# Gated networks of a two-block transformer kernel: a second chunk through seven block products for eight, weight sums made in DRAM, one stream of weight blocks

## The chip, the cores and the metric

One NeuronCore of a Trainium2 chip runs the whole program. The metric is device time in microseconds from start to end of one execution, taken as the median over runs. Engines are PE (TensorE), DVE (VectorE), ACT (ScalarE), POOL (GpSimd) and SP (SyncE, which only issues DMAs here).

## The reference, cut to what matters

Two transformer blocks are applied to 512 tokens of width 1024. The first has a mixer, a cross-attention and a two-matrix network (D_FF 4096). The second has a gated network, a token mixer with two kinds of attention, and a second gated network. The change touches the gated networks:

```python
def swiglu(h, w1, w3, w2):                     # w1, w3: 1024 x 2816, w2: 2816 x 1024
    return (jax.nn.silu(h @ w1) * (h @ w3)) @ w2

h = rmsnorm(x, ffn1_norm[l])
x = x + 0.5 * swiglu(h, ffn1_w1[l], ffn1_w3[l], ffn1_w2[l])
...
h = rmsnorm(x, ffn2_norm[l])
x = x + 0.5 * swiglu(h, ffn2_w1[l], ffn2_w3[l], ffn2_w2[l])
return rmsnorm(x, final_norm[l])
```

All is float32. The kernel makes each product of three reduced-precision products: an operand is split in a high part (rounded to fp32r) and a low part (the rest), and high*high, high*low and low*high are added in PSUM.

## The kernel before, in words

**Layout.** Activations lie with features on the partitions: 8 tiles (KT) of 128 features by 512 tokens (T). `h` is the running sum; `xh`/`xl` and `ah`/`al` are two pairs of high and low parts, one for a layer's input and one for its hidden values. A **panel** is 1024 rows by 256 columns (PC) of a weight matrix, 1 MB. SP loads it into one of two halves of `raw`, ACT rounds it into `wh` (`conv`, or `hi` by halves), and DVE subtracts to get `wl` (`conv`, `lo`); panel p uses half p % 2 of all three. PE then runs 2 output tiles x 8 k tiles x 3 matmuls of 512 columns (`panel_t`). SP issues a load when the panel two before has been converted (`conv_done`), ACT converts when PE has finished the panel two before (`lin_done`). Every engine works through its own list in program order and waits on counting semaphores.

**Order of panels.** `P0` numbers the panels: fqk, fv, gqk, gv, gr (mixer of block one, woven with attention), xk and xv (keys and values of the memory, 256 tokens wide, so that PE needs half the columns for them), wout, xq, xo, mlp, ffn1, then `SEQ` (block two's mixer, q0 ... v3, nq0 ... ga3, woven with attention), mnsa, wout2, ffn2. Between the fourth and fifth load of xv and wout, SP also issues the two reloads of `h` (L608, L610), 1 MB each, on the same queue.

**A gated network.** The 2816 hidden columns are cut in a tail of 768 and two chunks of 1024. The tail is done by plain panels: 6 of w1 and w3, then 4 panels of w2 with 6 k tiles. Each chunk r = 1, 2 is a **phase**: four groups, then four plain panels of w2 (three of them counted here for the last one in ffn2; the fourth is woven into the end of the kernel).

**A group** does 256 columns of w1 and of w3 together as a 2 x 2 block product in seven products for eight. A block is 512 rows by 256 columns of weights (4 k tiles) against 256 tokens. A product is 2 output tiles x 4 k tiles x 3 = 24 matmuls of 256 columns.

```python
B11, B21, B22, T1, T2, T3, T4 = range(7)
A11, A12, A22, S3, S1, S2, S4 = range(7)
PRODUCTS = [(A11, B11, 0), (A12, B21, 2), (S2, T2, 0), (S3, T3, 1), (S1, T1, 0), (A22, T4, 1), (S4, B22, 0)]
```

The third number says which of the group's three PSUM banks takes the product; two groups alternate between the banks `ps0, ps1, pt1` (shown by the profile as score, score, turned) and `po0, po1, pt0` (mix, mix, turned). T1 to T4 are sums of token quarters, made once for a network (`token_parts`, kept in `XS_h`, `XS_l`). S1 to S4 are sums of weight quarters, made for each group by DVE in the raw buffers (`sum_1` to `sum_4`, `add_up`, L3022), between the conversions of the blocks (`block_high` on ACT, `block_low` on DVE). SP loads four quarters of 512 KB for each group (L630), into `raw` or into the spare room of `xl_f` or `al_f`. ACT copies partial results out (`kept`), DVE adds them (`made_11`, `made_22`, `made_21`), ACT applies Silu, DVE multiplies (`gate`), and both write the high and low parts of the hidden values. In `in_turn`, product 6 of a group comes after product 0 of the next.

GpSimd has no work in this kernel, and no DMA comes from its queue.

Of the kernel before, what the change touches and what calls it, by code (L numbers as in the profile page):

```python
# [11 lines left out]
PART = 128  # L12
# [26 lines left out]
for name_, count_ in (("small", 1), ("fqk", 4), ("fv", 2), ("gqk", 2), ("gv", 2), ("gr", 2), ("xk", 4), ("xv", 4),  # L39
                      ("wout", 4), ("xq", 4), ("xo", 4), ("mlp", 20), ("ffn1", 18),  # L40
                      ("mix2", 32), ("mnsa", 8), ("wout2", 4), ("ffn2", 18)):
    P0[name_] = at
    at += count_
# [59 lines left out]
MLP0 = {"mlp": 2, "ffn1": 2 + 8 + 24, "ffn2": 2 + 8 + 24 + 22}  # L103
ML_S0 = MLP0["ffn1"]
# [7 lines left out]
for name_, chunks_, groups_ in (("mlp", 3, 2), ("ffn1", 2, 4), ("ffn2", 2, 4)):  # L112
    for r_ in range(1, chunks_ + 1):
        PHASES[name_, r_] = (at, groups_, P0[name_] + (8 if name_ == "mlp" else 10) + 4 * (r_ - 1))
        at += groups_
# [160 lines left out]
def build(nc, d, out):  # L276
    ctx = ExitStack()
    with ctx:
# [3399 lines left out]
```

## Time and profile before

| what | us |
|---|---|
| median of 3 runs | 2136.93 (2136.85 to 2138.73) |
| the profiled execution | 2138.95 |
| its span, first to last instruction | 2137.2 |
| PE busy | 2118.8 (99%) |
| DVE busy | 1372.5 (64%) |
| ACT busy | 1032.6 (48%) |

The span is what the rows below lie in. The profiled execution took 1.75 us more than its span and lies 2.0 us above the median. Busy PE means that a matmul is in flight: matmuls overlap, so a matmul of 256 columns is shown at 281 ns though the next one starts some 118 ns later. How long a stretch takes is read from its ends, not from these durations.

### The profile page before, as it was taken

To read this page: it belongs to the slowest core of one execution; us is meant where nothing else is said; L and a number is where in the kernel's file an instruction comes from. 1 tells how busy PE (TensorE), PEld (TensorE's weight loads), DVE (VectorE), ACT (ScalarE), POOL (GpSimd) and SP (SyncE) were. 2 spreads that over 40 slices of the span, in tenths; PEclk is the share of its full clock that TensorE was granted. 3 is DMA by queue.
4 is the path that set the end of the run, shared out by engine and by line. 5 is a ranking of instruction groups with operands and counts; after the bars stand their busy time and mean duration, and the time that the engine had idled before them with its cause. 6 is when DMAs were issued, how large, how long until landed. Compare 5 with 4: busy or idle time off the path is not lost.

```text
span 2137.2 us, 32530 instructions
## 1 busy us (share of the span) xinstructions
PE 2118.8 (99%) x13100; PEld 1819.8 (85%) x13100; DVE 1372.5 (64%) x2281; ACT 1032.6 (48%) x1738; POOL 0.2 (0%) x4
## 2 busy tenths in 40 slices
PE   9999999999999999999999999999999999999999
PEld 7888988888998988898988888887777888899997
DVE  4664663467664767775856777647776356686674
ACT  6654545543533543453543565546666234354344
POOL 0000000000000000000000000000000000000000
PEclk9999999999999999999999999999999999999999
DMA  5121522133233132424323622321111233242421
GB/s 189 60 80 60 180 97 80 40 99 118 80 119 118 61 98 84 138 75 138 100 80 98 181 83 82 98 84 50 40 37 40 79 99 99 87 139 72 138 68 71
DMA packets 190920, 199.74 MB, mean 93 GB/s; under 512 B 8481, under 2 KB 185778, under 8 KB 190258
## 3 DMA queue, kind: packets, MB, share of 16 engines
q1 hardware_dynamic: 190770, 197.66, 29.2%
q8 instruction: 104, 1.70, 0.3%
q14 instruction: 46, 0.38, 0.1%
HBM read 188.73 MB, written 2.10 MB: 89 GB/s over the span
## 4 chain that ended last, share of the span: by engine, by line
PE 93%; DVE 3%; ACT 2%; issue 1%; DMA 1%; SPq 0%; DVEq 0%; ACTq 0%
PE lin L733 20%; PE lin L735 19%; PE lin L734 19%; PE mix L1279 3%; PE mix L1280 3%; PE mix L1281 3%; PE score L1279 3%; PE score L1280 3%; PE score L1281 3%; PE turned L834 3%; PE score L929 3%; PE mix L943 2%; PE turned L1279 1%; PE turned L1280 1%; PE turned L1281 1%
## 5 line engine op out<-in xcount | busy, mean ns | idle before, releaser
L733 PE MATMUL lin<-xh,wh 128*128 128x512 f32 (+1 forms) x1032 | 407.5, 395 | 1.7 <-DVE wl L2494 1.2
L735 PE MATMUL lin<-xh,wl 128*128 128x512 f32 (+1 forms) x1032 | 394.8, 383 | 0.0
L734 PE MATMUL lin<-xl,wh 128*128 128x512 f32 (+1 forms) x1032 | 393.7, 382 | 0.0
L733 PE MATMUL lin<-ah,wh 128*128 128x512 f32 (+1 forms) x788 | 308.5, 392 | 1.4 <-DVE al L2499 0.6
L735 PE MATMUL lin<-ah,wl 128*128 128x512 f32 (+1 forms) x788 | 306.0, 388 | 0.0
L734 PE MATMUL lin<-al,wh 128*128 128x512 f32 (+1 forms) x788 | 305.9, 388 | 0.0
L2488 DVE TENSOR_TENSOR wl<-raw,wh 128x2048 fp32r<-128x2048 f32 x85 | 194.8, 2292 | 123.7 <-ACT wh L1595 123.7
L733 PEld LDWEIGHTS lin<-xh,wh 128*128 128x128 f32 x1032 | 194.2, 188 | 45.4 <-issue 9.6
L735 PEld LDWEIGHTS lin<-xh,wl 128*128 128x128 f32 x1032 | 194.0, 188 | 39.0
L734 PEld LDWEIGHTS lin<-xl,wh 128*128 128x128 f32 x1032 | 194.5, 188 | 34.8 <-issue 1.0
L1595 ACT ACTIVATE wh<-raw 128x2048 fp32r<-128x2048 f32 x85 | 162.0, 1906 | 113.4 <-PE lin L735 106.4
L733 PEld LDWEIGHTS lin<-ah,wh 128*128 128x128 f32 x788 | 148.0, 188 | 33.2 <-issue 1.6
L735 PEld LDWEIGHTS lin<-ah,wl 128*128 128x128 f32 x788 | 147.9, 188 | 30.7
L734 PEld LDWEIGHTS lin<-al,wh 128*128 128x128 f32 x788 | 148.0, 188 | 30.1 <-issue 0.2
L2494 DVE TENSOR_TENSOR wl<-raw,wh 128x1024 fp32r<-128x1024 f32 x90 | 109.5, 1220 | 40.4 <-ACT wh L1602 39.9
L2602 DVE CUSTOM_DVE_ANT_0 arena<-score,cst 128x128 f32<-128x128 f32 (+2 forms) x224 | 97.6, 486 | 58.0 <-PE score L929 46.6
L1692 ACT ACTIVATE arena<-arena,negm 128x128 f32<-128x128 f32 (+2 forms) x224 | 122.8, 555 | 3.1 <-DVE negm L2602 3.0
L1680 ACT ACTIVATE arena<-turned 128x512 f32<-128x512 f32 (+1 forms) x128 | 68.8, 582 | 112.5 <-PE turned L834 112.2
L1602 ACT ACTIVATE wh<-raw 128x1024 fp32r<-128x1024 f32 x90 | 94.1, 1052 | 36.1 <-PE lin L735 23.8
L1280 PE MATMUL mix<-arena_r,wh 128*128 128x256 f32 x352 | 98.9, 281 | 0.0
L1281 PE MATMUL mix<-arena_r,wl 128*128 128x256 f32 x352 | 98.9, 281 | 0.0
L1279 PE MATMUL mix<-arena_r,wh 128*128 128x256 f32 x352 | 98.9, 281 | 0.0
(434 smaller groups left out, 4301.1 us busy)
## 6 DMA issues: line engine op xcount, KB each, us to landing
raw<-in_w_in_dram SPq DMA_DIRECT2D x38, 1024.0 KB, 5.3
raw<-in_ffn_w_dram SPq DMA_DIRECT2D x28, 1024.0 KB, 5.2
raw<-in_mlp_w_dram SPq DMA_DIRECT2D x20, 1024.0 KB, 5.2
raw<-in_ffn_w_dram SPq DMA_DIRECT2D x32, 512.0 KB, 4.8
raw<-in_xattn_wkv_dram SPq DMA_DIRECT2D x8, 1024.0 KB, 5.3
raw<-in_w_out_dram SPq DMA_DIRECT2D x8, 1024.0 KB, 5.3
xl_f<-in_ffn_w_dram SPq DMA_DIRECT2D x16, 512.0 KB, 6.0
al_f<-in_ffn_w_dram SPq DMA_DIRECT2D x16, 512.0 KB, 5.5
```

The lines of the kernel that those rows point to most:

```text
L733: nc.tensor.matmul(o, w[0], x[0], start=first, stop=False)
L734: nc.tensor.matmul(o, w[0], x[1], start=False, stop=False)
L735: return nc.tensor.matmul(o, w[1], x[0], start=False, stop=last)
L1279: nc.tensor.matmul(o[:, c, :], left_h[:, k, cols], XS_h[:, b, k, :], start=begins, stop=False, skip_group_check=True)
L1280: nc.tensor.matmul(o[:, c, :], left_h[:, k, cols], XS_l[:, b, k, :], start=False, stop=False, skip_group_check=True)
L1281: mm = nc.tensor.matmul(o[:, c, :], left_l[:, k, cols], XS_h[:, b, k, :], start=False, stop=k == HT - 1, skip_group_check=True)
L1595: nc.scalar.activation(wh[:, p % 2], raw[:, p % 2], ACT.Copy).then_inc(hi_done, 1)
L1602: nc.scalar.activation(wh[:, p % 2, :, cols], raw[:, p % 2, :, cols], ACT.Copy).then_inc(hi_half[c], 1)
L1692: op = nc.scalar.activation(PB[:, s % 2, a, col:col + nk], SM[:, a, col:col + nk], ACT.Exp, bias=negm[:, at:at + 1], scale=-1.0, accum_out ...
L2488: nc.vector.tensor_tensor(wl[:, p % 2], raw[:, p % 2], wh[:, p % 2].bitcast(F32), ALU.subtract).then_inc(conv_done, 1)
L2494: nc.vector.tensor_tensor(wl[:, p % 2, :, cols], raw[:, p % 2, :, cols], wh[:, p % 2, :, cols].bitcast(F32), ALU.subtract).then_inc(conv_d ...
L2602: op = nc.vector.tensor_tensor_reduce(out=SM[:, a, col:col + nk], in0=ps[a][:, col:col + nk], in1=mask, scale=scale, scalar=BIG, op0=ALU.a ...
```

## The change

1. **The down product of the first chunk** (w2 rows of chunk 1, all 1024 output columns) is no longer four plain panels but two sets of seven block products: quarters of w2 are 4 k tiles by 512 columns. Its right-hand blocks are the hidden values, in quarters B11, B21, B22 (`hidden_at`) and sums T1 to T4, which DVE makes as the values come (`turned`) and ACT and DVE split (`U_T`, `turned_low`). Each product's PSUM is added to `h` straight away by DVE (`added`), with scale 0.5 or -0.5.
2. **Weight sums** S1 to S4 are no longer made by DVE. A new program on GpSimd makes them in DRAM, for all 1024 (or 512) columns of a chunk at once: a copy, then DMAs that add to what lies there (`accum_op`). Eight steps for each of UP, DOWN and LAST, 24 for each network, each waiting for the one before (`su`). A step moves 2 MB (UP, LAST) or 1 MB (DOWN). Those of ffn1 begin when PE has finished all panels before fv, those of ffn2 when it has finished all before nq0.
3. **One stream.** The ten sets (4 UP, 2 DOWN, 4 LAST) are one list of 70 blocks. Every block, sums too, is loaded by SP (512 KB), into six raw buffers in turn, and split into a ring of five (`ring_at`; one of the five is a new place in the arena). Then come the four (or three) plain panels of the second chunk.
4. Panels fall from 18 to 14 for each gated network, and several counts are renumbered.

```diff
+UP, DOWN, LAST = range(3)
+SETS = [(UP, i_) for i_ in range(4)] + [(DOWN, i_) for i_ in range(2)] + [(LAST, i_) for i_ in range(4)]
+STREAM = in_turn(4) + [(4, n_) for n_ in (0, 3, 1, 2, 4, 5)] + [(5, 0), (4, 6)] + [(5, n_) for n_ in (3, 2, 1, 4, 5)]
+STREAM += [(6, 0), (5, 6)] + [(i_ + 6, n_) for i_, n_ in in_turn(4)[1:]]
+BLOCKS, RINGS, RAWS = len(STREAM), 5, 6
+SUM_STEPS = 24
+SUMS_FROM = {"ffn1": P0["fv"], "ffn2": P["nq0"]}
...
         @block.sync
...
-                for r in range(1, 3):
-                    phase(name, r, p0 + 6, w2[:, (r - 1) * KT:r * KT])
+                p = p0 + 10
+                for b in range(BLOCKS):
+                    if b >= RAWS:
+                        sp.wait_ge(st_l, block_count(name, b - RAWS))
+                    elif b < 2:
+                        sp.wait_ge(lin_done, 2 * (p0 + 6))
+                    else:
+                        sp.wait_ge(conv_done, p if b < 4 else p - 1)
...
+                    if sums_ready(name, b):
+                        sp.wait_ge(su, sums_ready(name, b))
+                    sp.dma_start(raw_at(name, b), block_source(name, b)).then_inc(landed_b, 16)
...
+        @block.gpsimd
+        def _(pool):
+
+            def step(n, dst, src, **kw):
+                if n:
+                    pool.wait_ge(su, 16 * n)
+                pool.dma_start(dst, src, **kw).then_inc(su, 16)
+
+            for name in GATED:
+                pool.wait_ge(lin_done, 2 * SUMS_FROM[name])
+                for what in (UP, DOWN, LAST):
+                    n = SUM_STEPS * GATED.index(name) + 8 * what
+                    a11, a12, a21, a22 = quarters(name, what)
+                    s3, s1, s2, s4 = sums_of(name, what)
+                    step(n, s3, a11)
+                    step(n + 1, s3, a21, accum_op=ALU.add)
+                    step(n + 2, s1, a21)
+                    step(n + 3, s1, a22, accum_op=ALU.add)
+                    step(n + 4, s2, s3)
+                    step(n + 5, s2, a22, accum_op=ALU.add)
+                    step(n + 6, s4, s2)
+                    step(n + 7, s4, a12, accum_op=ALU.add)
...
         @block.tensor
...
+            def stream(name):
...
+                for b, (s, n) in enumerate(STREAM):
+                    what = SETS[s][0]
+                    if s == 4 and n in (3, 1):
+                        continue
+                    if s == 4 and n == 0:
+                        pe.wait_ge(ml_lo, hidden_count(name, 2, 3))
+                        for n_ in (0, 3, 1):
+                            pe.wait_ge(st_l, block_count(name, AT[s, n_]))
+                            bank_free(s, n_)
+                            part(s, n_, range(HT - 1))
+                        pe.wait_ge(ml_lo, hidden_count(name, 3, 3))
+                        for n_ in (0, 3, 1):
+                            part(s, n_, [HT - 1]).then_inc(st_q, 1)
+                        continue
+                    pe.wait_ge(st_l, block_count(name, b))
+                    if n in (0, 1, 3):
+                        bank_free(s, n)
+                    elif what == DOWN:
+                        pe.wait_ge(st_c, event_count(name, s, {2: 0, 4: 2, 5: 3, 6: 4}[n]))
...
+                    part(s, n, range(HT)).then_inc(st_q, 1)
...
-                phase(name, 1, Y)
-                phase(name, 2, Y, 3 if name == "ffn2" else 4)
+                stream(name)
+                outputs(p0 + 10, Y, lambda k: pe.wait_ge(ml_lo, hidden_count(name, 6 + k // 2, 2)), 3 if name == "ffn2" else 4)
...
         @block.scalar
...
+                for b, (s, n) in enumerate(STREAM):
...
+                    elif what == UP and n == 6:
+                        high(hidden_at(name, 0, B22)[:, i, :], E_ur[:, 1, :], s, 2)
+                        act.wait_ge(st_a, turned_count(name, i, 4))
+                        nc.scalar.activation(US[name][0][1][:, 0:4, i, :], U_T, ACT.Copy).then_inc(ml_hi, 1)
...
+                def turned(i):
+                    dve.wait_ge(ml_e, 2 * MLP_G + gate_count(name, i, 2))
...
+                    nc.vector.tensor_tensor(U_T[:, T3 - T1, :], b12, b22, ALU.subtract).then_inc(st_a, 1)
...
+                    nc.vector.tensor_tensor(U_T[:, T2 - T1, :], U_T[:, T3 - T1, :], b11, ALU.subtract).then_inc(st_a, 1)
...
+                    nc.vector.tensor_tensor(U_T[:, T4 - T1, :], b21, U_T[:, T2 - T1, :], ALU.add).then_inc(st_a, 1)
+                    nc.vector.tensor_tensor(U_T[:, 0, :], b11, b12, ALU.subtract).then_inc(st_a, 1)
...
+                def added(s, n, i):
...
+                    dve.wait_ge(st_q, product_count(name, s, n))
...
+                    nc.vector.scalar_tensor_tensor(hk, half_bank(s, at), scale, hk, ALU.mult, ALU.add).then_inc(st_c, 1)
...
+                for b, (s, n) in enumerate(STREAM):
+                    what, i = SETS[s]
+                    up = what != DOWN
+                    if not up:
+                        added(s, n, i)
...
+                    if b + RINGS < BLOCKS:
+                        stream_low(name, b + RINGS)
```

**DVE, from the fourth UP set to the first DOWN set.** Before, at the end of the first phase (L3136 is a gate, L3067 a `made`, L2499 a low part, L2488 a panel's low part, L2551 the add into `h` from a plain panel):

```order
L3067 TENSOR_TENSOR arena<-mix,arena 128x512 [waits st_e,st_q]
L3136 TENSOR_TENSOR arena<-arena 128x512 [waits ml_s,st_c]
L2499 TENSOR_TENSOR al<-arena,ah 128x2x256 [waits ml_hi]
L3136 TENSOR_TENSOR arena<-arena 128x512 [waits ml_s,st_c]
L2499 TENSOR_TENSOR al<-arena,ah 128x2x256 [waits ml_hi]
L2488 TENSOR_TENSOR wl<-raw,wh 128x2048 [waits hi_done]
L2551 SCALAR_TENSOR_TENSOR h<-lin,h 128x512 [waits lin_done] x2
```

Now, at the same place (L3365 is the gate, L3376 to L3381 are `turned`, L2722 a low part, L3399 is `added`):

```order
L3365 TENSOR_TENSOR arena<-arena 128x512 [waits ml_s,st_c]
L3376 TENSOR_TENSOR arena<-arena 128x256 [waits ml_lo,ml_e]
L3378 TENSOR_TENSOR arena<-arena 128x256 [waits st_a]
L3380 TENSOR_TENSOR arena<-arena 128x256 [waits st_a]
L3381 TENSOR_TENSOR arena<-arena 128x256
L2722 TENSOR_TENSOR xl<-arena,xh 128x256 [waits ml_hi]
L2722 TENSOR_TENSOR al<-arena,ah 128x4x256 [waits ml_hi]
L2722 TENSOR_TENSOR wl<-raw,wh 128x1024 [waits st_h]
L3399 SCALAR_TENSOR_TENSOR h<-score,h 128x2x256 [waits st_q]
L2722 TENSOR_TENSOR wl<-raw,wh 128x1024 [waits st_h]
L3399 SCALAR_TENSOR_TENSOR h<-score,h 128x2x256 [waits st_q]
L2722 TENSOR_TENSOR wl<-raw,wh 128x1024 [waits st_h]
```

Four small sums and a wide low part stand behind the last gate, and in the DOWN sets each product's add into `h` is followed by the low part of a block that is used five products later.

**POOL, its whole list before:**

```order
L3667 ISA
L3667 MEMSET const-float32-0.0 128x1
L3667 MEMSET const-float32-1.0 128x1
L3667 MEMSET const-bfloat16-1.0 128x1
L3667 MEMSET const-uint8-127 128x1
```

Now, behind the same five, the steps of ffn1 up to the first of LAST (`up_sums_ffn_0` are the sums of the first chunk, `down_sums_ffn` those of w2):

```order
L876 DMA up_sums_ffn_0<-in_ffn_w_2_dram 128x4x1024 [waits lin_done]
L876 DMA up_sums_ffn_0<-in_ffn_w_2_dram 128x4x1024 [waits su] x3
L876 DMA up_sums_ffn_0<-up_sums_ffn_0 128x4x1024 [waits su]
L876 DMA up_sums_ffn_0<-in_ffn_w_2_dram 128x4x1024 [waits su]
L876 DMA up_sums_ffn_0<-up_sums_ffn_0 128x4x1024 [waits su]
L876 DMA up_sums_ffn_0<-in_ffn_w_2_dram 128x4x1024 [waits su]
L876 DMA down_sums_ffn<-in_ffn_w_2_dram 128x4x512 [waits su] x4
L876 DMA down_sums_ffn<-down_sums_ffn 128x4x512 [waits su]
```

Each step is one DMA from DRAM to DRAM and waits for all of the one before. None of them waits for, or holds up, a compute engine directly; they share the DMA engines with SP's loads.

## Rows read from the trace of the kernel before

**Rows 1.** The page: busy engines, and the queue of SP's loads.

```profile
PE 2118.8 (99%) x13100; PEld 1819.8 (85%) x13100; DVE 1372.5 (64%) x2281; ACT 1032.6 (48%) x1738; POOL 0.2 (0%) x4
...
q1 hardware_dynamic: 190770, 197.66, 29.2%
```

**Rows 2.** Waits of PE: line, whom it waited for, us, times, longest.

```profile
PE score L1279 <- DVE wl L2499: 1.2, 2, 0.8
```

**Rows 3.** Windows: us, PE, PEld, DVE, ACT, POOL busy, clock, DMA share, GB/s.

```profile
884.00:964.00 80.00, 79.19 (x673) 78.98 (x672) 65.44 (x68) 41.24 (x51) 0.00 (x0) 1.00 0.27 85
1007.60:1087.30 79.70, 79.70 (x673) 79.70 (x672) 62.97 (x66) 40.32 (x50) 0.00 (x0) 1.00 0.27 85
1879.00:1960.30 81.30, 80.87 (x674) 80.65 (x673) 65.18 (x67) 41.19 (x51) 0.00 (x0) 1.00 0.27 84
2003.90:2083.60 79.70, 79.70 (x674) 79.70 (x673) 62.95 (x66) 40.41 (x50) 0.00 (x0) 1.00 0.27 85
964.00:1007.60 43.60, 43.60 (x195) 36.08 (x194) 20.51 (x19) 11.52 (x10) 0.00 (x0) 1.00 0.42 136
```

**Rows 4.** Groups of instructions between 1007.6 and 1087.3 us (the second phase).

```profile
L2499 DVE TENSOR_TENSOR wl<-xl_f,wh 128x1024 fp32r<-128x1024 f32 x10 | 12.2, 1220 | 3.6 <-ACT wh L2055 3.6
L2055 ACT ACTIVATE wh<-xl_f 128x1024 fp32r<-128x1024 f32 x10 | 10.5, 1054 | 9.1 <-DVE xl_f L3022 4.9 <-PE mix L1281 3.6 <-PE score L1281 0.7
L3022 DVE TENSOR_TENSOR xl_f<-xl_f 128x1024 f32<-128x1024 f32 x8 | 9.8, 1220 | 0.1
```

**Rows 5.** The line of one token sum: durations in ns.

```profile
L3001 DVE TENSOR_TENSOR arena<-arena x12: 425/425/426, 476.3 to 1846.4; 128x256 f32<-128x256 f32 x12
```

**Rows 6.** Timeline where the second phase's last product ends: start us, us, engine.

```profile
1087.32 0.39 PE L733 MATMUL lin<-ah,wh 128*128 128x512 f32 x1
...
1087.52 0.60 ACT L2133 ACTIVATE arena<-mix 128x512 f32<-128x512 f32 x1 [6.15 <-PE mix L1281]
...
1089.27 0.68 DVE L3136 TENSOR_TENSOR arena<-arena 128x512 f32<-128x512 f32 x1
```

**Rows 7.** Windows in the memory's values and the output projection.

```profile
222.00:272.00 50.00, 50.00 (x399) 49.07 (x398) 29.83 (x32) 24.73 (x36) 0.00 (x0) 1.00 0.63 211
246.60:258.10 11.50, 11.50 (x98) 11.50 (x97) 2.85 (x2) 5.50 (x6) 0.00 (x0) 1.00 0.96 345
```

**Rows 8.** Timeline of SP, ACT and DVE there.

```profile
246.13 0.37 SPq L577 DMA_DIRECT2D raw<-in_xattn_wkv_dram  x1
246.54 0.58 SPq L608 DMA_DIRECT2D h<-in_x_t_dram  x1
247.16 0.43 SPq L610 DMA_DIRECT2D h<-in_x_t_dram  x1
254.10 0.38 SPq L577 DMA_DIRECT2D raw<-in_w_out_dram  x1
...
261.37 1.90 ACT L1595 ACTIVATE wh<-raw 128x2048 fp32r<-128x2048 f32 x1
267.13 1.91 ACT L1595 ACTIVATE wh<-raw 128x2048 fp32r<-128x2048 f32 x1
...
263.30 2.29 DVE L2488 TENSOR_TENSOR wl<-raw,wh 128x2048 fp32r<-128x2048 f32 x1 [3.47 <-ACT wh L1595]
```

**Rows 9.** DMA between 1719 and 1726 us: queues, and the issue with its us to landing.

```profile
q8 instruction: 1, 0.02, 1.7%
...
raw<-in_w_out_dram SPq DMA_DIRECT2D x1, 1024.0 KB, 6.7
```

**Rows 10.** The page: DMA issues, KB each, median us to landing.

```profile
raw<-in_w_out_dram SPq DMA_DIRECT2D x8, 1024.0 KB, 5.3
...
arena<-arena SPq DMA_DIRECT2D x104, 64.0 KB, 2.0
```

**Rows 11.** Timeline of ACT where the new steps' start conditions are met.

```profile
70.64 1.91 ACT L1595 ACTIVATE wh<-raw 128x2048 fp32r<-128x2048 f32 x1
...
1362.57 1.05 ACT L1602 ACTIVATE wh<-raw 128x1024 fp32r<-128x1024 f32 x1
```

More of the change, by code:

```diff
@@ L101 @@
 HEAD_TILES = [0, 4, 1, 5, 2, 6, 3, 7]
[L103 to L104 removed]
+MLP0 = {"mlp": 2, "ffn1": 2 + 8 + 24, "ffn2": 2 + 8 + 24 + 26}
+GATE0 = {"ffn1": 0, "ffn2": 22}
 TAIL = 3
@@ L111 @@
 PHASES, at = {}, 0
[L112 to L115, printed above, removed]
+for r_ in range(1, 4):
+    PHASES["mlp", r_] = (at, 2, P0["mlp"] + 8 + 4 * (r_ - 1))
+    at += 2
 GROUPS = at
@@ new lines, in build, with quarters, sums_of @@
+        down_sums = {name: nc.dram_tensor(f"down_sums_{name}", (4, HT * PART, 2 * PC), F32, kind="Internal").ap() for name in GATED}
+        def quarters(name, what):
+            w1, w3, w2 = ffw[name]
+            if what == DOWN:
+                return [w2[:, e:KT:2, c * 2 * PC:(c + 1) * 2 * PC] for c in range(2) for e in range(2)]
+            r = what // LAST
+            return [w[:, e * HT:(e + 1) * HT, r * D:(r + 1) * D] for w in (w1, w3) for e in range(2)]
+        def sums_of(name, what):
+            store = down_sums[name] if what == DOWN else up_sums[name, what // LAST]
+            return [tiles(store[k]) for k in range(4)]
@@ new lines, in own, with raw_at, ring_at @@
+        def own(name):
+            return (P0[name] + 10) % 2
+        def raw_at(name, b):
+            at = b % RAWS
+            if at < 2:
+                return ((ah_f, al_f) if name == "ffn2" else (xh_f, xl_f))[at][:, 3]
+            side = own(name) if at >= 4 else 1 - own(name)
+            return raw[:, side, at % 2 * HT:(at % 2 + 1) * HT, :]
+        def ring_at(name, b):
+            at = b % RINGS
+            if at == 0:
+                return RING_h, RING_l
+            side = own(name) if at < 3 else 1 - own(name)
+            at = (at - 1) % 2
+            return tuple(x[:, side, at * HT:(at + 1) * HT, :] for x in (wh, wl))
@@ L549, in build, with hidden_at, set_banks, half_bank @@
+        def hidden_at(name, side, b):
+            left, turned = US[name][side]
+            return left[:, b] if b < T1 else turned[:, b - T1]
+        def set_banks(s):
+            return ((ps[0], ps[1], pt[1]), (po[0], po[1], pt[0]))[s % 2]
+        def half_bank(s, at):
+            return set_banks(s)[at].rearrange("p (a n) -> p a n", a=2)
         block = ctx.enter_context(nc.Block())
@@ L1296, in phase, with outputs @@
+            def outputs(p, Y, made, panels=4):
                 s = p % 2
@@ L3210, in rest @@
                 last()
-            chunk("mlp", p + 4, 1.0, {0: third, 1: fourth, 2: fifth})
+            early, later, last = first_blocks(PHASES["mlp", 1][0])
+            residual(p + 4, None, None, 1.0, 2, {0: third, 1: fourth, 2: fifth, 5: early, 6: later})
+            last()
             for r in range(1, D_FF // D):
```

339 lines of the change are left out of this document (213 added, 126 removed).

## The prediction

> **What bounds the kernel now.** I read the page first: PE is busy 99% of the span, DVE 64%, ACT 48%, and SP's queue uses 29.2% of the DMA engines [rows 1]. So the time is PE's list of matmuls plus the gaps in it, and anything else counts only where it makes PE wait. Next the waits of PE: inside the gated networks there are just two, together 1.2 us, both for the low part of a block at the start of a first phase [rows 2]. Then the windows by stage: a phase of 28 products (672 matmuls of 256 columns) takes 80.0, 79.7, 81.3 and 79.7 us, and the four plain panels between two phases (192 matmuls of 512 columns) take 43.6 us [rows 3]. That is 79.7 / 672 = 0.1186 us and 43.6 / 192 = 0.2271 us for a matmul. DVE is busy 63 to 65 us in 80, so it is the engine nearest to PE there. The DMA engines are busy 27% in a phase.
>
> **The sum for PE's list.** Removed for each network: 192 matmuls of 512 columns. Added: 14 products x 24 = 336 matmuls of 256 columns, 336 x 0.1186 = 39.85 us. The stream has 70 x 24 = 1680 matmuls, 199.25 us at that pace. Before, the same work took 80.0 + 43.6 + 79.7 = 203.3 us in ffn1 and 81.3 + 43.6 + 79.7 = 204.6 us in ffn2. So -4.05 and -5.35, together **-9.4 us**. This takes with it the two waits of [rows 2], which I expect to go: block 0 no longer waits for the last tail panel's buffer and there are no sums to make between the first blocks. About 1 us of it is that ffn2's first phase ran slower than the others; I don't know why, and count on the usual pace.
>
> **DVE's list.** A sum of a block costs 1.22 us; there were 4 for each group, 16 in a phase, so 32 x 1.22 = 39 us of DVE goes for each network [rows 4]. Added are 4 UP sets x 4 small sums x 0.425 us [rows 5] and the wide low part, 1.22 us. DVE gets lighter, but that was hidden under PE and gives nothing.
>
> **The turn from UP to DOWN.** Where the fourth UP set ends, the hidden values' sums are late next. Before, after a last product ACT starts Silu 0.20 us after PE went on, takes 0.60, and a gate takes 0.68 [rows 6]. The chain now: 0.2 + 0.6 + 0.7 + 4 x 0.43 for `turned` + 1.05 for ACT's copy of `U_T` + 1.22 for DVE's low part [rows 4 to 6] + some 0.2 for hand-overs = 5.7 us. PE meanwhile does 3 products without their last k tile, 54 x 0.1186 = 6.4 us. So no wait, with 0.7 us to spare; if the cover were gone it would cost up to 1 us a network.
>
> **Behind the turn there is one.** In the first DOWN set product 4 uses the PSUM bank of product 2 and follows it directly (0, 3, 1, 2, 4, 5), so PE must wait for `added` of product 2. DVE is behind then. I count from the end of the last UP product: `turned_low` ends at 5.6, the next block's low part at 6.75. Products 0, 3, 1 end at 7.1, 7.8, 8.55, nearly at once. DVE then does three times `added` (0.65, as the 512-element gate of [rows 6]) and a block's low part (1.15 back to back), whose high part ACT can only start when the product has freed the ring: 7.3 to 9.6, to 11.35, to 13.1. `Added` of product 2 ends at 13.8, but PE ended that product at 8.55 + 2.85 = 11.4. Wait: 2.4 us, twice, **+4.8 us**. Bounds: 1.0 us each if DVE is free at once (hand-over and 0.7), 3.5 each if every block adds another 0.3. In the other DOWN set a product of another set lies between the two. From there to the plain panels, `conv(p)` waits for product 67 of 70, 5.7 us before the end, and needs 1.9 + 2.3 us [rows 8]: hidden.
>
> Both together: -9.4 + 4.8 = **-4.6 us**, if the DMAs cost nothing.
>
> **The steps on GpSimd.** They are off every engine, so their price is only what they take from SP's loads. The trace has no DRAM-to-DRAM DMA and none that adds. The nearest row for data is 345 GB/s in a stretch where the engines are 96% busy [rows 7], for the fixed part 2.0 us of a 64 KB DMA [rows 10]. A copied step of 2.1 MB: 6.1 + 2.0 = 8.1 us. For an adding step the lower bound is the same (8.1), the upper three passes (read what is there, read what is added, write): 20.3. I take two passes, 14.2. With halves for DOWN: UP 4 x 22.3 = 89, DOWN 4 x 13.1 = 52, LAST 89, in all 230 us. The steps of ffn1 begin at 70.6, when PE has finished the panels ahead of fv [rows 11]: LAST would run from 212 to 301 us. At the lower bound all 24 take 170 us and end at 240, a bit later because the loads share.
>
> The Trainium skill (Collectives: The Full Stack, "The bandwidth ceiling") says that a reducing DMA needs two source reads and so runs at half a copy's rate; that is what I took, and no row here shows it. Its page DMA: Bandwidth & Descriptors ("Anatomy of one DMA") gives 2.0 us + bytes / 436 GB/s for a GpSimd DMA; with that and the halved rate LAST would run from 189 to 263 us, and the sum below would end 2.6 us lower.
>
> **Who is hurt.** A load hardly matters where its data lie ready long before conversion. The one stretch where they don't is xk, xv and wout: the panels of the memory need half the columns, and the DMA engines are busy 63% over 50 us and 96% from 246.6 to 258.1 [rows 7]. SP issues at 246.13, 246.54, 247.16 and 254.10 four MB in a row [rows 8]; 4.2 MB at 345 GB/s and 2.0 us fixed end at 260.3. The last of them is wout's first panel: ACT converts it at 261.37, DVE ends at 265.6, PE starts it when it has finished the one before, 267.13, where ACT starts the next conversion [rows 8]. So slack is 1.1 + 1.5 = 2.6 us. As the DMA engines have no free time there, what the steps move is added one for one. I take one adding step, 12.2 us of data: 12.2 - 2.6 = 9.6, and with what the xv panels before it lose **+10.5 us**. Bounds: nothing (steps over, or the arbiter favours SP), and two adding steps of three passes with the copy between, 2 x 18.3 + 6.1 = 42.7, less the 18.5 us that the engines are idle in those 50: 24.
>
> That a load suffers from another queue is in the trace: one packet of the instruction queue, 1.7% of 16 engines x 7 us = 1.9 us on one engine, made a load land after 6.7 us where the median is 5.3 [rows 9, 10]. The skill's DMA page ("Queues, rings and completion order") says that each engine takes turns between queues by packets. With SP's 1 KB against 4 KB rows of the sums, SP would get a small share while a step runs, which leans to the upper half of my bounds.
>
> ffn2's steps begin at 1362.57 [rows 11] and would end near 1593, with loads that wait for conversion anyway, long before 1879 [rows 3]. I count 0 for them, up to 10 us if a load queued ahead of the small rotations' DMAs is late.
>
> **Sum:** -9.4 + 4.8 + 10.5 = +5.9 us. Against the profiled execution's 2138.95 this is 2144.8; that execution lies 2.0 above the median of the runs shown, so I forecast 2142.8.
>
> **Rivals.** About 0.2% (4.3 us) is what a measurement of this kernel can tell from no change.
> - *A, forecast: the steps of LAST collide with the loads of xv and wout, for more than 8.9 us.* For it: 63% and 96% DMA share. Time 2141.2 to 2157, likeliest 2142.8. Chance 0.43.
> - *B: they collide, but cost only 3 to 8.9 us,* because adding steps have long idle parts in which SP catches up. 2135.3 to 2141.2, say 2138. Chance 0.19.
> - *C, the other side: no collision that counts.* It decides itself at 246.13: 24 steps in 175 us, 7.3 us each, while my lower bound is 170 us. Or SP's small packets pass ahead. Then -4.6 us: 2132.3; with a DOWN wait of 1.0 us each 2129.5. Chance 0.32, of which 0.22 below 2132.7 and 0.10 just within 0.2%.
> - *D: adding is far slower.* LAST's first sum of ffn2 is loaded about 33 products into the stream, 1879 + 94 = 1973. From 1362.57 that is 25 us for each step, 2.6 times what I took (230 / 24 = 9.6). Beyond that PE waits for sums, and the steps lie over all loads of both halves: +25 us and more, 2162 and up. Chance 0.06.
>
> **Chances.** Slower: A 0.43 + D 0.06 = 0.49. Faster: 0.22 of C, and 0.04 of B where the DOWN wait is smaller too: 0.26. Same: 0.25. Range: below 2129 lie some 0.07 (C with a faster pace of matmuls), above 2160 D and the end of A, 0.10. So 2129 to 2160. The forecast case alone is 2141 to 2157.
>
> **What would show it.** In the trace of the changed kernel: the stream at 199 us plus one gap of about 2.4 us before the fifth product of the first DOWN set, ended by DVE's `added`; no gap at its start; none at the turn. GpSimd's DMAs from 70 to about 300 us and from 1363 to 1600. Loads of xv and wout that land after 8 to 17 us instead of 5.3, and PE idle between 235 and 285 us by about 10 us. I am wrong if PE is not idle there, if the steps end before 246, or if the gaps in the stream sum to another size.

## The result, and the profile after

The changed kernel takes **2161.98 us** (median of 4 runs, 2160.51 to 2163.58) against 2136.90 (4 runs, 2136.85 to 2138.73): ratio 1.0115, 95% interval 1.0098 to 1.0133. It is 25 us slower, where I had forecast 5.9 and a range up to 2160. The profiled execution took 2162.04 with a span of 2159.5, 22.3 more than the span of before.

The page of the changed kernel: busy engines, queues (packets, MB, share of 16 engines), DMA issues (KB each, median us to landing; the 24 are 8 copies and 16 additions).

```profile
PE 2119.8 (98%) x13388; PEld 1833.4 (85%) x13388; DVE 1348.2 (62%) x2289; ACT 1053.8 (49%) x1766; POOL 49.0 (2%) x52
...
q1 hardware_dynamic: 222578, 229.12, 33.6%
q0 software_dynamic: 23296, 83.89, 15.9%
...
up_sums_ffn<-in_ffn_w_dram POOLq DMA_DIRECT2D x24, 2048.0 KB, 14.1
...
up_sums_ffn<-up_sums_ffn POOLq DMA_DIRECT2D x8, 2048.0 KB, 9.4
```

PE has 288 matmuls more than in [rows 1], short ones for long ones, and is busy 1.0 us longer. The span grew by 22.3, so the loss is idle time, and what the idle time does to PE's busy time. Its waits in the changed kernel: line, whom it waited for, us, times, longest.

```profile
PE lin L900 <- DVE wl L2711: 9.2, 2, 5.5
PE score L1460 <- DVE h L3399: 4.7, 2, 2.3
PE turned L1001 <- DVE arena L3643: 4.1, 1, 4.1
PE lin L900 <- DVE arena L2753: 2.9, 1, 2.9
```

The pair of waits in [rows 2] is gone. In its place stand four kinds. The waits behind L2711 and L2753 end at 244.01, 269.54 and 282.51 us: VectorE is named, but it had waited, through ScalarE, for a load. L3399 is `added` in the first DOWN set of each network. L3643 lies at 1403, which nothing in my sum had. The windows show what the page can't (us, PE, PEld, DVE, ACT, POOL busy, clock, DMA share, GB/s):

```profile
235.00:300.00 65.00, 52.90 (x334) 49.05 (x333) 22.20 (x23) 20.82 (x27) 4.76 (x5) 0.89 1.02 319
...
244.00:247.00 3.00, 2.99 (x14) 3.00 (x15) 3.00 (x5) 0.00 (x0) 0.00 (x0) 0.50 0.49 199
250.00:253.00 3.00, 3.00 (x27) 3.00 (x26) 0.93 (x1) 0.47 (x1) 0.00 (x0) 1.00 1.12 252
993.40:995.70 2.30, 0.04 (x1) 0.00 (x0) 2.30 (x4) 1.06 (x1) 0.00 (x0) 1.00 0.74 241
996.00:999.00 3.00, 3.00 (x27) 3.00 (x27) 0.84 (x2) 0.03 (x1) 0.00 (x0) 1.00 0.86 279
1998.30:2001.30 3.00, 3.00 (x16) 3.00 (x16) 0.06 (x1) 0.00 (x1) 0.00 (x0) 0.50 1.01 311
```

In 235 to 300 us the DMA engines have no free time (1.02; 0.63 and 0.96 in [rows 7]), and PE is idle for 12.1 us of 65. Right behind the first wait the granted clock is 0.50, the lower of the two levels (1.2 GHz): 14 matmuls in 3 us instead of 27. PE counts as fully busy there. So a wait costs more than its length: three waits of 12.1 us in all cost 18.4. The same at 1998, behind a wait of 2.3 us; behind the like wait at 995.7 the clock stayed at 1.00.

Where the time went I read from the moments at which PE ends the same panel in two traces. Each column is the difference to the kernel before, in us; the last line is the difference of the spans. What a column shows in its first line stands there from the first panel on, so it is an offset of the start. The execution that all columns are taken from lies 2.0 us above the median of its kernel, so the last line flatters every variant by up to that much: e9 is 10.0 lower there and 7.9 in the medians.

| end of | before, at | changed | e8 | e1 | e3 | e7 | e9 |
|---|---|---|---|---|---|---|---|
| xk's third panel | 238 | +0.3 | -0.2 | -0.3 | -0.6 | -0.4 | -0.4 |
| xk's last panel | 244 | +4.8 | +4.7 | -0.3 | +3.9 | +5.1 | -0.4 |
| xv's last panel | 267 | +10.3 | +11.1 | -0.3 | +10.9 | +5.1 | -0.4 |
| wout's second panel | 290 | +18.7 | +19.3 | -0.3 | +18.9 | +5.1 | -0.4 |
| ffn1's tail (the stream starts) | 884 | +18.6 | +19.2 | +4.2 | +18.7 | +5.0 | -0.5 |
| ffn1 and the next panels | 1137 | +16.4 | +19.0 | +2.1 | +14.0 | +0.3 | -5.2 |
| SEQ up to nq0 | 1375 | +17.9 | +18.8 | +3.7 | +15.3 | +0.8 | -3.8 |
| the first delta attention panel | 1415 | +23.8 | +19.8 | +10.6 | +16.9 | +0.8 | -3.8 |
| ffn2's tail (the stream starts) | 1879 | +24.6 | +21.1 | +10.6 | +16.9 | +1.0 | -3.6 |
| the span | 2137.2 | +22.3 | +19.6 | +8.2 | +10.4 | -5.4 | -10.0 |

The changed kernel: 18.4 lost beside xv and wout (4.5 by the end of xk, 5.5 in xv, 8.4 in wout's first panel), 2.3 gained by ffn1, 1.5 lost at about 1200, 5.9 at 1400, 0.8 at about 1570, 2.3 gained by ffn2.

**The first place.** GpSimd's issues, then ACT and SP, in the changed kernel (start us, us):

```profile
226.49 1.26 POOL L876 DMA_DIRECT2D down_sums_ffn<-in_ffn_w_dram  x1 [5.42 <-DMA down_sums_ffn<-down_sums_ffn]
236.49 0.76 POOL L876 DMA_DIRECT2D up_sums_ffn<-in_ffn_w_dram  x1 [8.74 <-DMA down_sums_ffn<-in_ffn_w_dram]
247.44 1.25 POOL L876 DMA_DIRECT2D up_sums_ffn<-in_ffn_w_dram  x1 [10.19 <-DMA up_sums_ffn<-in_ffn_w_dram]
263.69 0.76 POOL L876 DMA_DIRECT2D up_sums_ffn<-in_ffn_w_dram  x1 [15.00 <-DMA up_sums_ffn<-in_ffn_w_dram]
276.48 1.24 POOL L876 DMA_DIRECT2D up_sums_ffn<-in_ffn_w_dram  x1 [12.03 <-DMA up_sums_ffn<-in_ffn_w_dram]
...
258.94 26.67 SPq L704 DMA_DIRECT2D raw<-in_w_out_dram  x4
...
265.25 1.91 ACT L1800 ACTIVATE wh<-raw 128x2048 fp32r<-128x2048 f32 x1 [4.71 <-DMA raw<-in_xattn_wkv_dram]
278.18 1.91 ACT L1800 ACTIVATE wh<-raw 128x2048 fp32r<-128x2048 f32 x1 [10.29 <-DMA raw<-in_w_out_dram]
```

LAST begins at 236.5, not at 212, and its fourth step is issued at 276.5. Wout's first panel, issued at 258.94, lands at 278.2. The DMA view of this load, in the kernel before (issued at 254.10) and in the changed one (KB, us to landing):

```profile
raw<-in_w_out_dram SPq DMA_DIRECT2D x1, 1024.0 KB, 6.5
raw<-in_w_out_dram SPq DMA_DIRECT2D x1, 1024.0 KB, 19.2
```

ACT had waited 10.3 us for it. Three steps lie over this one load, one of them issued ahead of it and two while it runs; I had counted one. Xv's last load takes 14.3 us where it took 5.6, and ACT waits 4.7 us for it.

How hard a step crowds SP's loads differed with its kind. Queues in the changed kernel (packets, MB, share of 16 engines), first from 252 to 258.9 us, inside an adding step, then from 263.7 to 276.5, a copied one. SP has three loads outstanding in the first stretch and two or more in the second:

```profile
q0 software_dynamic: 316, 1.29, 95.1%
q1 hardware_dynamic: 184, 0.19, 10.0%
...
q1 hardware_dynamic: 1406, 3.17, 63.0%
q0 software_dynamic: 528, 2.10, 39.8%
```

Beside the adding step SP's queue (q1) moves 0.19 MB in 6.9 us, beside the copy 3.17 MB in 12.8. That stretch is the worst of the adding step; over all of it, 247.4 to 263.7 us, SP's queue has 38.8%.

**The second place,** at 1399 us: SP's swap of the first sparse query tile's halves (64 KB DMAs), VectorE behind it, PE behind that.

```profile
1393.66 2.41 SPq L825 DMA_DIRECT2D arena<-arena  x4
...
1398.21 0.69 DVE L3524 TENSOR_TENSOR arena<-arena,cst 128x512 f32<-128x512 f32 x1 [5.36 <-DMA arena<-arena]
...
1403.32 0.66 PE L1001 MATMUL turned<-cst,arena 128*128 128x128 f32 x4 [4.10 <-DVE arena L3643]
```

And from the DMA view of that moment (KB each, us to landing):

```profile
arena<-arena SPq DMA_DIRECT2D x1, 64.0 KB, 5.8
```

A 64 KB DMA takes 5.8 us beside an adding step, 2.0 in [rows 10]. VectorE's instruction that needs it stands ahead of the one that PE needs, and PE waits 4.1 us for a value that has nothing to do with the swap.

### The profile page after: what moved, and what is told of

It reads as the page before. It is cut to its first block, busy times and chain, and to the rows that moved or that the text cites. A ratio compares the mean times of both kernels' runs of the same rounds, so it can differ in the third digit from the quotient of the medians.

```text
span 2159.5 us, 33285 instructions
## 1 busy us (share of the span) xinstructions
PE 2119.8 (98%) x13388; PEld 1833.4 (85%) x13388; DVE 1348.2 (62%) x2289; ACT 1053.8 (49%) x1766; POOL 49.0 (2%) x52
## 4 chain that ended last, share of the span: by engine, by line
PE 89%; DVE 4%; DMA 3%; ACT 2%; issue 1%; SPq 0%; DVEq 0%; ACTq 0%
PE lin L900 18%; PE lin L902 17%; PE lin L901 17%; PE mix L1461 3%; PE mix L1462 3%; PE mix L1460 3%; PE score L1460 3%; PE score L1461 3%; PE score L1462 3%; PE turned L1001 3%; PE score L1096 2%; PE mix L1110 2%; DMA raw<-in_w_out_dram 1%; PE turned L1461 1%; PE turned L1462 1%
## 5 line engine op out<-in xcount | busy, mean ns | idle before, releaser
L900 PE MATMUL lin<-xh,wh 128*128 128x512 f32 (+1 forms) x968 | 384.1, 397 | 5.8 <-DVE arena L2753 2.9
L902 PE MATMUL lin<-xh,wl 128*128 128x512 f32 (+1 forms) x968 | 371.2, 383 | 0.0
L901 PE MATMUL lin<-xl,wh 128*128 128x512 f32 (+1 forms) x968 | 370.0, 382 | 0.0
L900 PE MATMUL lin<-ah,wh 128*128 128x512 f32 x724 | 284.9, 393 | 6.9 <-DVE wl L2711 5.5
L902 PE MATMUL lin<-ah,wl 128*128 128x512 f32 x724 | 282.0, 390 | 0.0
L901 PE MATMUL lin<-al,wh 128*128 128x512 f32 x724 | 281.9, 389 | 0.0
L2711 DVE TENSOR_TENSOR wl<-raw,wh 128x2048 fp32r<-128x2048 f32 x77 | 176.5, 2292 | 127.8 <-ACT wh L1800 127.8
L2722 DVE TENSOR_TENSOR wl<-raw,wh 128x1024 fp32r<-128x1024 f32 x88 | 107.0, 1222 | 47.5 <-ACT wh L2340 46.3
L2717 DVE TENSOR_TENSOR wl<-raw,wh 128x1024 fp32r<-128x1024 f32 x90 | 109.5, 1221 | 42.2 <-ACT wh L1807 41.7
L1807 ACT ACTIVATE wh<-raw 128x1024 fp32r<-128x1024 f32 x90 | 94.1, 1052 | 46.4 <-PE lin L902 26.0
L2340 ACT ACTIVATE wh<-raw 128x1024 fp32r<-128x1024 f32 x74 | 77.7, 1055 | 61.1 <-PE score L1462 19.5
L900 PE MATMUL lin<-wh,xh 128*128 128x256 f32 x320 | 93.3, 292 | 3.8 <-DVE wl L2711 3.8
```

What stands on the lines that cost most here:

```text
L900: nc.tensor.matmul(o, w[0], x[0], start=first, stop=False)
L901: nc.tensor.matmul(o, w[0], x[1], start=False, stop=False)
L902: return nc.tensor.matmul(o, w[1], x[0], start=False, stop=last)
L2711: nc.vector.tensor_tensor(wl[:, p % 2], raw[:, p % 2], wh[:, p % 2].bitcast(F32), ALU.subtract).then_inc(conv_done, 1)
L2717: nc.vector.tensor_tensor(wl[:, p % 2, :, cols], raw[:, p % 2, :, cols], wh[:, p % 2, :, cols].bitcast(F32), ALU.subtract).then_inc(conv_d ...
L2722: nc.vector.tensor_tensor(dst, full, hi.bitcast(F32), ALU.subtract).then_inc(done, 1)
```

## The experiments

Theory 1: the loss is that of place, sums beside loads that have no slack. Theory 2: the sums cost as much wherever they lie. Theory 3: the new stream of products costs it. Theories 1 and 2 are told apart by moving sums, 3 by leaving them out. The differences by place that I name are those of the table or read in the same way.

### e1: ffn1's sums later

```diff
-SUMS_FROM = {"ffn1": P0["fv"], "ffn2": P["nq0"]}
+SUMS_FROM = {"ffn1": P0["xq"], "ffn2": P["nq0"]}
```

> Only the start of ffn1's 24 sums moves, from the second panel of FoX's v projection (70 us) to the xattn query projection (about 340 us), behind the stage in which PE waited. Theory 1 (place): the 18.4 us that the changed kernel falls behind between 235 and 300 us come from the loads of xv, wout and xq standing in line with the sums, so they go and nothing takes their place, because the loads of xo and of the mlp's panels have more slack: 2143.5, 2140 to 2146. Theory 2 (the sums cost wherever they lie): the same number of bytes meets other loads; the loss moves to 400 to 600 us and the time stays at 2158 to 2163. Theory 3 (the new stream of products is what costs, the waits at 240 to 280 being its effect by some other way): no change, 2162.

2148.37 (2147.12 to 2150.71), before 2138.18 (19 runs), ratio 1.0050 (1.0033 to 1.0067): above the 2140 to 2146 that I expected. The 18.4 us are gone to the last tenth (-0.3 at 290 us). But 4.7 came back at 540 us, so theory 1 holds with a part of theory 2 in it: the sums met the mlp's first group loads, which have no slack either. The loss at 1400 was 6.9 this time.

### e2: no sums

```diff
-        @block.gpsimd
-        def _(pool):
...
-                    if sums_ready(name, b):
-                        sp.wait_ge(su, sums_ready(name, b))
-                src = sums_of(name, what)[SUM[a] - 1]
+                src = quarters(name, what)[SUM[a] - 1]
```

> The 48 sum steps and the waits for them are left out; the blocks that were sums are read straight from a quarter of the weight instead, so the output is not the reference's, but PE, VectorE, ScalarE and SP's own loads do all the work of the changed kernel. Theory 1: all of the loss is DMA traffic, what is left is the shorter list of products (-9.4) and the two 2.3 us waits in the first set of the down product with up to 1.7 us of half clock behind the second: 2132 to 2135, 2 to 5 us below the kernel before. Theory 3 (the new stream costs more than its matmuls): above 2140. If the waits for the sums themselves (blocks late for the stream) cost anything it shows as a difference between this run and the one with both sets of sums moved.

2135.44 (10 runs), before 2138.18, ratio 0.9988 (0.9979 to 0.9997): 0.4 above the 2132 to 2135 that I expected, 2.7 below the kernel before. The span is 2132.4, 4.8 below before, where my sum without the DMAs had -4.6; 1.4 of the 4.8 is a slow phase in the trace of before (see e8). Theory 3 falls.

### e3: the order of the first DOWN set

```diff
-[(4, n_) for n_ in (0, 3, 1, 2, 4, 5)]
+[(4, n_) for n_ in (0, 3, 1, 2, 5, 4)]
```

> In the first set of the down product, products 4 and 5 change places, so that the one that adds to the bank of product 2 no longer follows it at once. Everything else is the changed kernel. Theory 1 (my step on VectorE's wait): both waits of 2.3 us on h go, and so does the 3.4 us stretch of half clock at 1998 us: 4.6 to 6.5 us less than the changed kernel, 2155.5 to 2157.5. Rival: the VectorE chain of sixteen instructions behind the end of the up product is what is late, and the wait only moves to product 5 or to the next set: within 1 us of the changed kernel, 2161 to 2162.5.

2153.66 (2150.21 to 2155.86), ratio 1.0071 (1.0056 to 1.0086). Both waits are gone, and nothing stands in their place. Ffn1 gives 4.7 (18.7 to 14.0) instead of 2.3. The median is 8.3 below the changed kernel, 1.8 more than I expected at most. The profiled execution is the fastest of the four (2150.21), and it lost 1.6 at 1399 us instead of 5.9; what the other three lost there, no trace shows. E11 prices the order without this. The DVE rows of the changed kernel show the wait:

```profile
992.07 1.22 DVE L2722 TENSOR_TENSOR wl<-raw,wh 128x1024 fp32r<-128x1024 f32 x1
993.20 0.68 DVE L3399 SCALAR_TENSOR_TENSOR h<-turned,h 128x512 f32<-128x512 f32 x1
993.80 1.22 DVE L2722 TENSOR_TENSOR arena_r<-raw,arena_r 128x1024 fp32r<-128x1024 f32 x1
994.93 0.68 DVE L3399 SCALAR_TENSOR_TENSOR h<-score,h 128x512 f32<-128x512 f32 x1
...
995.76 0.36 PE L1460 MATMUL score<-ah,wh 128*128 128x256 f32 x1 [2.33 <-DVE h L3399]
```

VectorE works without a gap, an addition and a low part in turn, and PE gets its bank back when the fourth addition ends.

### e4: both sums later, and the new order

```diff
+SUMS_FROM = {"ffn1": P0["xq"], "ffn2": P["wda0"]}
+[(4, n_) for n_ in (0, 3, 1, 2, 5, 4)]
```

> Three edits in one: ffn1's sums from the xattn query projection, ffn2's sums two panels later (from the first output panel of the delta attention instead of the first query panel of the sparse attention, so that the swap of the first query tile is ahead of them), and the order of the down product as in the run before. Theory 1: 18.4 + about 6 + 4.6 to 6.5 us less than the changed kernel: 2131 to 2133.5, 4 to 6 us below the kernel before. Theory 2 (sums cost wherever they lie): 2150 or more. If ffn2's sums meet the later swaps in the same way, the second part stays and it is 2137 to 2139.

2134.11 (10 runs), ratio 0.9981 (0.9972 to 0.9990): 4.1 below the kernel before, where I expected 4 to 6, and 0.6 above the expected 2131 to 2133.5. PE's longest wait:

```profile
PE score L1440 <- DVE wl L2722: 3.6, 1, 3.6
```

This is the mlp's first group, at 540 to 544 us: 5.0 with the half clock behind it, 4.7 in e1. The wait at 1399 is gone (+0.0 there).

### e7: only ffn1's LAST steps later

The rest as in e4, but ffn1's sums begin at `P0["fv"]` as in the change.

```diff
+                    if name == "ffn1" and what == LAST:
+                        pool.wait_ge(lin_done, 2 * P0["xq"])
```

> The order of the down product of e3 and ffn2's start of e4, but ffn1's sums start where the change put them (70 us); only the eight steps of its LAST set are held back to the xattn query projection (about 335 us). The eight UP and eight DOWN steps lie between 70 and 235 us, where the changed kernel lost 0.3 us; the LAST steps lie between 335 and about 425, ahead of the mlp's first group loads at 510 to 518, which cost e4 its one stall (3.9 us and a 3.4 us stretch of half clock, 4.8 in the milestones). Theory 1 (place: it is a question of which loads the sums lie beside): e4 less 4.8, so 2129.3, 2128 to 2131. Theory 2 (a sum costs the same anywhere): 2134, and a stall in the xattn stage between 335 and 425.

2134.70 (11 runs), ratio 0.9984 (0.9976 to 0.9993). My expectation of 2129.3 was a miss: the mlp's wait went, but a wait at 240 stayed, which with the half clock behind it cost 5.5 us (-0.4 to +5.1):

```profile
PE lin L902 <- DVE arena L2755: 3.8, 1, 3.8
```

I had read "0.3 lost until 235" as no harm, but the harm of the last DOWN step shows only behind 235. (The 0.3 is no loss at all, but the offset of the start.) Rows of e7's timeline, and its DMA view for that load (KB, us to landing):

```profile
227.13 1.26 POOL L876 DMA_DIRECT2D down_sums_ffn<-in_ffn_w_dram  x1 [5.72 <-DMA down_sums_ffn<-down_sums_ffn]
...
229.13 22.50 SPq L704 DMA_DIRECT2D raw<-in_xattn_wkv_dram  x4
...
239.05 1.06 ACT L1809 ACTIVATE wh<-raw 128x1024 fp32r<-128x1024 f32 x1 [7.20 <-DMA raw<-in_xattn_wkv_dram]
```

```profile
raw<-in_xattn_wkv_dram SPq DMA_DIRECT2D x1, 1024.0 KB, 9.9
```

The first load of xv is issued at 229.13, 2 us behind one adding step of 1 MB, and takes 9.9 us. ACT converts it in the moment it lands. PE doesn't wait for this panel yet: ACT and VectorE work in order, and behind the conversion stands the emptying of the PSUM bank that PE needs in xk's last panel. One step in flight beside one load without slack is enough.

### e5: only ffn2's sums later

```diff
+SUMS_FROM = {"ffn1": P0["fv"], "ffn2": P["wda0"]}
```

> The changed kernel with one number changed: ffn2's sums start two panels later, after the swap of the first query tile of the sparse attention has been issued. Theory 1: the 4.4 us wait at 1399 us and the half clock behind it go: 5 to 6 us less than the changed kernel, 2156 to 2157. Rival (the swap of the second or third tile is held up instead): 2160 to 2163.

2153.76 (2151.36 to 2157.08), ratio 1.0077 (1.0063 to 1.0090). At 1415 us nothing is lost (+17.2 ahead of it and behind), and up to 1575 us only 0.6 more, so the later swaps are hardly hurt. The median lies 2.2 us under the least that I expected and 8.2 under the changed kernel; the wait at 1399 is worth 5.9 in the profiled execution.

### e6: copies in the place of additions

```diff
-                    step(n + 1, s3, a21, accum_op=ALU.add)
+                    step(n + 1, s3, a21)
...
```

> Every adding transfer becomes a plain copy of the same bytes at the same place in the chain, so the output is not the reference's. It prices the adding itself. In the changed kernel a 2 MB step takes about 8 to 12 us as a copy and 14 to 16 as an addition. If the stalls come of the packets of the additions being slow, the chain of ffn1 ends by 260 to 290 us instead of 343, DMA share in 235 to 290 falls, and 6 to 15 of the 18.4 us come back: 2147 to 2156. Rival (it is the bytes and the queueing of any large transfer): the copies follow one another faster and crowd as much per microsecond, the loss between 235 and 270 stays and only what lies after the end of the chain is saved: 2156 to 2160.

2151.21 (2150.10 to 2157.26), ratio 1.0069 (1.0056 to 1.0083): inside the first range. GpSimd's last step of ffn1 is issued at 271.7 instead of 328.1. DMAs between 60 and 300 us:

```profile
up_sums_ffn<-in_ffn_w_dram POOLq DMA_DIRECT2D x12, 2048.0 KB, 9.2
...
raw<-in_w_out_dram SPq DMA_DIRECT2D x4, 1024.0 KB, 10.6
```

A copied step takes 9.2 us. An adding one takes 14.5 where little else runs (in e7 one is issued at 328.6 and the next step at 343.1). At 290 us e6 stands at +14.3 instead of +18.7. Without the offsets of the start that is 14.5 lost instead of 18.4, so only 3.9 came back there, less than the 6 to 15 that the first range rested on; the rest of the gain lies elsewhere (4.0 lost instead of 5.9 at 1400). So most of the loss doesn't need the adding; large copies crowd a load out too, as the rival had it, though not with its time and later in the stage (4.2 by the end of xv, 10.3 in wout's first panel).

### e8: the kernel before with the sums

```diff
+        @block.gpsimd
+        def _(pool):
...
+                    step(n, s3, a11)
+                    step(n + 1, s3, a21, accum_op=ALU.add)
...
```

> The kernel before, with the 48 sum steps on GpSimd's queue at the same two places, into DRAM that nobody reads. Products, stream of blocks and waits are those of before. Theory 1 (the whole of the loss is this traffic beside loads that the change did not touch): before plus 18.4 between 235 and 300, plus 2 to 7 at 1399, that is 2158 to 2165, with the same idle places of PE. Theory 3 (the new stream is at fault): 2138 to 2142. If it falls between, the rest belongs to the new stream.

2161.35 (2158.16 to 2164.53), before 2137.86, ratio 1.0115 (1.0099 to 1.0130): the ratio of the changed kernel. The waits lie in the same places (end of wout's second panel +19.3), only the one at 1400 is small in this trace (1.0). With e2 this shows that the transfers are the cause: they alone cost 23.5 in the median, the stream alone gives 2.7. The two add up to +20.8 where the change has +25.1; the losses at 1400 differ from trace to trace, and I can't say what else is in the 4.3 us between.

E8 shows one thing more. It has the products of the kernel before, but its first phase of ffn2 takes 79.8 us where [rows 3] have 81.3. The window of that phase in e8:

```profile
1900.30:1980.10 79.80, 79.16 (x673) 78.94 (x672) 65.10 (x67) 41.10 (x52) 0.00 (x0) 1.00 0.27 86
```

So some 1.4 us of what every variant gains by ffn2 in my table (+21.1 to +19.6 here) is a slow phase in the trace of before, and no effect of an edit.

### e9 and e10: a pause in ffn1's sums

Both have e4's order and start of ffn2's sums, and ffn1's sums begin at `P0["fv"]`. In e10 the pause is ahead of step 12.

```diff
+                if n == 14:
+                    pool.wait_ge(lin_done, 2 * P0["xq"])
```

> As e7, but ffn1's sums are held back two steps sooner: fourteen steps (eight UP, six DOWN) run from 70 us and are done by about 220, the last two DOWN steps and the eight LAST steps wait for the xattn query projection (319 us). In e7 the last DOWN addition was issued at 227.1 and the first load of xv, issued at 229.1 with no slack at all, took 9.9 us where it takes 5.3 in the kernel before, and PE waited 4.1 us. Theory 1 (a load without slack beside one step in flight): this wait and its 3.4 us of half clock go, 5.3 us less than e7, profiled time about 2129, median 2129 to 2130; PE's longest idle place is then the 1.5 us at 1213 us that the kernel before has too. Rival (the load is late because of GpSimd's queue as such, or the ten steps after 319 us now reach a load of the mlp): 2133 to 2135.

> As e9 with twelve steps ahead of the pause and twelve behind it, which end about 25 us later, near 460 us, still ahead of the mlp's group loads at 510. Theory 1: the same as e9 within 0.7 us. If it is slower than e9 by more, the later half has reached loads that have no slack either.

e9: **2129.43** (2129.08 to 2129.92), before 2137.33 (15 runs), ratio 0.9960 (0.9946 to 0.9973). e10: 2128.96, ratio 0.9958 (0.9944 to 0.9971). Both are 8 us faster than the kernel before. In e9 the timeline and the DMA view of xv's first load, and the windows of the stage and of the ten later steps:

```profile
234.40 1.06 ACT L1809 ACTIVATE wh<-raw 128x1024 fp32r<-128x1024 f32 x1 [2.95 <-DMA raw<-in_xattn_wkv_dram]
```

```profile
raw<-in_xattn_wkv_dram SPq DMA_DIRECT2D x1, 1024.0 KB, 5.3
```

```profile
235.00:300.00 65.00, 65.00 (x411) 59.19 (x411) 35.89 (x37) 28.55 (x40) 0.00 (x0) 1.00 0.52 175
319.00:430.00 111.00, 108.81 (x541) 92.20 (x540) 47.63 (x123) 55.79 (x102) 9.31 (x9) 1.00 0.84 216
```

The load takes 5.3 again and PE isn't idle from 235 to 300. The ten steps that were moved make the DMA engines 84% busy from 319 to 430 us, and cost nothing there.

### e11: e9 with the old order

> As e9, with the down product's order of the change (product 4 right behind product 2). It prices the term of the wait on VectorE by itself, with no transfer in the way: two waits of 2.3 us over e9, and a stretch of half clock behind one or both of them at 1.5 us each (at 0.213 us a matmul where 0.120 is the pace at full clock, 15 matmuls instead of 28 fit in 3.4 us): 4.6 to 7.6 us over e9, 2134 to 2137. The sum on record had 4.8 for it. If it is under 3 us over e9, the gain of the new order is taken back elsewhere.

2136.07 (10 runs), ratio 0.9992 (0.9983 to 1.0001), 6.6 over e9; spans 2133.7 and 2127.2. Its waits, and windows before and behind the first:

```profile
PE score L1462 <- DVE h L3401: 4.7, 2, 2.3
```

```profile
970.50:973.50 3.00, 3.00 (x28) 3.00 (x27) 2.54 (x4) 2.65 (x3) 0.00 (x0) 1.00 0.61 178
977.50:980.50 3.00, 3.00 (x17) 3.00 (x16) 0.17 (x1) 0.00 (x0) 0.00 (x0) 0.51 0.92 301
1972.70:1975.70 3.00, 3.00 (x27) 3.00 (x26) 0.85 (x2) 0.00 (x0) 0.00 (x0) 1.00 0.81 263
```

Two waits of 2.3 and one stretch of half clock (17 matmuls for 28). With these, the new order decides whether this change is a gain that can be measured.

## Why the prediction was wrong

- **What bounds the kernel:** right. PE's list and its gaps explain every difference.
- **PE's list, -9.4:** in e9, which has no wait in either stream, ffn1 gives 4.7 (-0.5 to -5.2) and ffn2 with the end of the program 6.4 (-3.6 to -10.0), 11.1 in all. Right in kind, 1.7 too small; I had 4.05 and 5.35. The slow first phase of ffn2 is in both numbers with 1.3 to 1.4, and e8 shows that it is not the change's to give. I had taken it off in the sum and then took off the 2.0 us by which that execution lies above its median, so I probably counted it twice.
- **The turn, 0:** right. No wait there.
- **The DOWN wait, +4.8:** 4.7 of idle time by the profile, at the product I had named. What was missing is the clock behind it: e11 shows 6.6 for the term.
- **The steps' times:** an adding step of 2 MB takes 14.5 where little else runs (forecast 14.2), a copied one 9.2 (8.1). But the sixteen steps of UP and DOWN took 166 us (70.3 to 236.5) where I had 141. The Trainium skill (Collectives: The Full Stack, "The bandwidth ceiling") says it of a ReduceScatter: its adding needs two source reads, and it runs at half the rate of an AllGather, which copies. The adding steps here agree roughly: with the 2.0 us fixed part taken off, 12.5 to 7.2 is 1.7.
- **SP's share beside a step:** "SP would get a small share while a step runs" holds for a part of an adding step (10.0% from 252 to 258.9 us, 38.8% over the whole), not beside a copied one (63.0%). E6 lost 14.5 without any adding step, so the share alone doesn't decide.
- **The step that failed: "I take one adding step ... +10.5".** The mechanism was the right one, the size was 18.4. Three things were off. I let one step collide with one load, but LAST came 24 us later than I had worked out (236.5, not 212), and its steps lay over the whole stretch to 300, three on the one load. I gave the xv panels 0.9 of the 10.5, and their loads cost 10.0: the first, which has no slack and lay beside the last DOWN step, 4.5, the last 5.5. And I turned DMA time into lost time one for one, when PE's clock fell to half behind each wait: 12.1 us idle became 18.4 lost. Wout's first load, for which I had 9.6, cost 8.4; that this is near is luck, as three steps lay over it and not one. My upper bound of 24 held the whole.
- **"I count 0 for them" (ffn2's steps):** 5.9 in the profiled execution, and in others 0.0 to 6.9 (e5, e8: 1.0, e3: 1.6, e6: 4.0, e1: 6.9). I had named the small rotation DMAs as the way it could cost, and had put no price in the sum.
- **Rivals:** A's mechanism is shown by e1, e2 and e8; its range ended at 2157 because of the above. B (3 to 8.9 us) and C (no collision) are out. D's place (over 2162) was nearly reached, but not by its mechanism: adding was as fast as I had it.

The sum with measured terms: -11.1 + 6.6 + 18.4 + 5.9 = +19.8, against +22.3 in the spans. What is left are 1.5 us at about 1200, 0.8 at about 1570 and the offset of 0.3 at the start. The one at 1200 is there in e1, e3, e9, e10 and e11 as well (1.3 to 1.7), less in e4, e7, e5, e2 and e6 (0.7 to 0.3) and not in e8. PE waits 1.3 us there for a low part. ScalarE, ahead of it, had waited 5.4 us for a load of `in_cmp_w` that took 7.7, against 4.0 and 6.3 before. No sum step runs then, and why the load is late stays open.

## What to carry to other kernels

Background transfers are priced by the slack of each load under them, not by their mean: list for each load when it lands and when it is converted, and keep large transfers away from those where the two are equal. Here one start condition, a pause and the order of two products turned 25 us of loss into 8 of gain. A chain of transfers needs a pause as well as a start, and small DMAs that an in-order engine waits for are as exposed as the large ones. Price a wait of PE by its length and by the clock behind it.

## What the runs showed of the hardware

- Behind a wait of PE of 2.3 us or more the granted clock often falls to half for some microseconds: 14 to 17 matmuls of 256 columns in 3 us, 27 or 28 at full clock. It doesn't always: of the two waits of 2.3 us in a kernel, the second drew it in the changed kernel, e1 and e5, the first in e2 and e11, neither in e6.
- A load of 1 MB takes 9.9 us beside one adding 1 MB step from GpSimd's queue (5.3 in the kernel before), another 19.2 beside three 2 MB steps (6.5 before); a 64 KB DMA takes 5.8 instead of 2.0.
- DRAM to DRAM, 2 MB: 9.2 us copied, 14.5 added.
- Beside an adding step SP's queue got 38.8% of the DMA engines' time and only 10.0% from 252 to 258.9 us, beside a copied one 63.0% from 263.7 to 276.5, with loads outstanding in both.
